# A two-stack transformer kernel: the order of VectorE's and ScalarE's work in mixer 1's tail, at mixer 2's entry and at the mixers' output

## The reference

```
x = x + 0.5 * rms(swiglu(rms(x)))          # feed-forward, width 2816
x = x + rms(token_mixing(rms(x) @ w_in))   # 6 heads band attention (A), 4 heads differential attention (B), 6 heads stick breaking (C)
x = x + 0.5 * rms(swiglu(rms(x)))
```

```
z = rms(h) @ w_in  ->  q, k, v, forget logit, a_val, a_gate, sc_b, sc_c, sc_x
y = [forgetting attention | silu(LN(dwconv31(a_val * sigmoid(a_gate)))) @ pw | sc_b * conv3(sc_c * sc_x)]
h = h + rms(head_rms(y) @ w_out);   h = h + rms(conv-swiglu(rms(h)))
```

## Time and profile before

| what | value |
|---|---|
| median of 3 runs | 3466.94 us (3461.26 to 3468.24) |
| the profiled execution's own time | 3464.3 us |
| its span | 3462.6 us |
| PE busy | 3362.6 us, 97% |
| DVE busy | 1761.5 us, 51% |
| ACT busy | 1413.3 us, 41% |
| POOL busy | 292.6 us, 8% |
| chain that ended last | PE 89%, DVE 5%, ACT 3% |
| mean granted TensorE clock | 0.99 |

### The profile page before, as it was taken

One profiled execution on the slowest core, in us unless ns is written; L12 is line 12 of the kernel. 1 busy time (PEld: TensorE's weight loads), 2 busy tenths in 40 slices (PEclk: granted clock), 3 DMA queues, 4 the chain that ended last, 5 costly groups with the idle time before them and its releaser, 6 DMA issues.

```text
span 3462.6 us, 52727 instructions
## 1 busy us (share of the span) xinstructions
PE 3362.6 (97%) x21230; PEld 2933.6 (85%) x21230; DVE 1761.5 (51%) x2408; ACT 1413.3 (41%) x2396; POOL 292.6 (8%) x159
## 2 busy tenths in 40 slices
PE   8999999899999999999899999999999999999999
PEld 7887876688889888876688888879999988799998
DVE  4443556554425442556554425745665267366643
ACT  3232445442224322446433224465443345654332
POOL 0000022100000000022100001210000022100000
PEclk9999999999999999999999999999999999999999
DMA  3333321223333332311223332112323322122222
GB/s 110 91 100 125 104 61 55 68 79 92 96 95 89 97 94 95 104 58 53 68 82 94 94 98 76 50 53 68 91 91 95 101 56 55 46 80 91 91 92 86
DMA packets 330735, 287.46 MB, mean 83 GB/s; under 512 B 9697, under 2 KB 326201, under 8 KB 330581
## 3 DMA queue, kind: packets, MB, share of 16 engines
q1 hardware_dynamic: 329444, 283.85, 27.3%
q10 hardware_dynamic: 1137, 1.42, 0.1%
HBM read 283.10 MB, written 5.27 MB: 83 GB/s over the span
## 4 chain that ended last, share of the span: by engine, by line
PE 89%; DVE 5%; ACT 3%; DMA 1%; issue 1%; ACTq 0%; POOL 0%; SPq 0%; DVEq 0%
PE ps L607 22%; PE ps L608 22%; PE ps L609 21%; PE ps L658 3%; PE ps L660 3%; PE ps L659 3%; PE ps L719 2%; PE ps L1829 1%; PE ps L1831 1%; PE ps L1830 1%; DVE m_aconv L2269 1%; PE ps L1417 1%; PE ps L723 1%; PE ps L1441 1%; PE ps L1456 1%
## 5 line engine op out<-in xcount | busy, mean ns | idle before, releaser
L607 PE MATMUL ps<-xhi,whi 128*128 128x512 f32 (+2 forms) x3088 | 1067.5, 346 | 18.2 <-DVE m_aconv L2220 13.1
L608 PE MATMUL ps<-xlo,whi 128*128 128x512 f32 (+2 forms) x3088 | 1058.1, 343 | 0.0
L599 DVE TENSOR_TENSOR wlo<-raw,whi 128x1024 fp32r<-128x1024 f32 (+1 forms) x410 | 495.2, 1208 | 1100.7 <-ACT whi L592 1098.2
L609 PE MATMUL ps<-xhi,wlo 128*128 128x512 f32 (+2 forms) x3088 | 1054.3, 341 | 0.0
L592 ACT ACTIVATE whi<-raw 128x1024 fp32r<-128x1024 f32 (+1 forms) x493 | 512.1, 1041 | 1143.2 <-PE ps L609 1031.7
L607 PEld LDWEIGHTS ps<-xhi,whi 128*128 128x128 f32 x3088 | 584.6, 189 | 104.2 <-issue 16.8
L609 PEld LDWEIGHTS ps<-xhi,wlo 128*128 128x128 f32 x3088 | 583.2, 189 | 69.6
L608 PEld LDWEIGHTS ps<-xlo,whi 128*128 128x128 f32 x3088 | 584.1, 189 | 66.1 <-issue 0.5
L607 PE MATMUL ps<-hhi,whi 128*128 128x512 f32 (+2 forms) x1056 | 358.9, 340 | 0.4 <-issue 0.4
L608 PE MATMUL ps<-hlo,whi 128*128 128x512 f32 (+2 forms) x1056 | 358.1, 339 | 0.0
L609 PE MATMUL ps<-hhi,wlo 128*128 128x512 f32 (+2 forms) x1056 | 357.7, 339 | 0.0
(11 more groups left out here) (287 smaller groups left out, 5141.2 us busy)
## 6 DMA issues: line engine op xcount, KB each, us to landing
raw<-in_ffn_w_up_dram SPq DMA_DIRECT2D x176, 512.0 KB, 3.7
raw<-in_ffn_w_down_dram SPq DMA_DIRECT2D x120, 512.0 KB, 3.4
raw<-in_w_in_dram SPq DMA_DIRECT2D x94, 512.0 KB, 3.8
raw<-in_ffn_w_gate_dram SPq DMA_DIRECT2D x88, 512.0 KB, 3.7
raw<-in_w_out_dram SPq DMA_DIRECT2D x32, 512.0 KB, 3.4
raw<-in_ffn_w_down_dram SPq DMA_DIRECT2D x24, 256.0 KB, 2.7
tbias_scratch<-rev_scratch SPq DMA_DIRECT2D x1, 3072.0 KB
y<-tbias_scratch SPq DMA_DIRECT2D x6, 512.0 KB, 4.6
```

The lines of the kernel that those rows point to most:

```text
L599: eng.tensor_tensor(lo[:, 0:n], raw[slot][:, 0:n], hi[:, 0:n].bitcast(F32), ALU.subtract).then_inc(b.s.weights_split, 1)
L607: pe.matmul(o, wh, hi[:, t0:t0 + w], start=first, stop=False)
L608: pe.matmul(o, wh, lo[:, t0:t0 + w], start=False, stop=False)
L609: ins = pe.matmul(o, wl, hi[:, t0:t0 + w], start=False, stop=last)
```

## The change

1. Mixer 1: `OUT_FILL` gives step 29 one output tile less (3 to 2) and step 33 one more (0 to 1). `B_NORM` is 23, so sums, logarithms, product and hi part of the B norm are each one step earlier; the lo part is at B_NORM+5, step 28 (before: 27).
2. Mixer 1, DVE: the evacuations and outputs of steps 27 and 30 (`DEFER1`) are done one step later, behind that step's `probabilities`. In step 27 this is the evacuation of granule 23 (pair 7's values), in step 30 the outputs of pair 6.
3. The lo split of granule 25 moves from POOL to DVE, step 30.
4. `act_out`, all mixers: `next_hi(0)` comes after `act_yevac` of m=1, and no longer before it.
5. Mixer 2's entry, PE: granule 4 waits for one evacuation, granule 5 for two (before: three and four). DVE evacuates granules 1 to 3 ahead of the forget chain, and gives `a_gate_in` before the forget lo part, both after evac(4).
6. Mixer 2, DVE: step 2 has three taps (2 and 1), step 3 four (1 and 3); the last three taps come in step 12.

```diff
--- before.py
+++ after.py
@@ -136,9 +136,11 @@
 
 
 LAG1 = 2
-OUT_FILL = [3, 3, 2, 2, 2, 0]
+OUT_FILL = [3, 2, 2, 2, 2, 1]
 OUT_TILES = [(24, t) for t in range(8)] + [(25, t) for t in range(4)]
-B_NORM = 24
+B_NORM = 23
+
+DEFER1 = (27, 30)
 
 
 def schedule1():
@@ -206,7 +208,7 @@
 FILL2 = [13, 13, 13, 13, 12] * 3 + [11, 11, 10]
 
 DW_OPS = [(t, c) for t in range(TAPS) for c in range(2)]
-DW_PER_STEP = 5
+DW_STEP = {2: (2, 1), 3: (1, 3)}
 
 
 def schedule2():
@@ -1132,10 +1134,11 @@
                 if j == nq * late - 1 and KIND[g][0] == "M":
                     for i in range(nq * late + (2 if KIND[g] == "M2" else 0), nq * DOWN_PAIRS):
                         hi_split(i)
-                    next_hi(0)
                 if j % nq == nq - 1:
                     act.wait_ge(b.s.granules_done, gb + j + 1 + CR)
                     act_yevac(act, b, g, j // nq, col)
+                if j == nq * late - 1 and KIND[g][0] == "M":
+                    next_hi(0)
             if KIND[g][0] == "F":
                 for i in range(nq * late + 2, nq * DOWN_PAIRS):
                     hi_split(i)
@@ -1717,16 +1720,19 @@
                     logits(st.sc)
                 if last is not None and KINDS[last // 4] == "B":
                     probabilities(last)
-                for g in st.done:
-                    if g < 24:
-                        evac(g)
-                for p_ in st.pairs:
-                    outputs(p_)
+                for n in ([n_step - 1] if n_step - 1 in DEFER1 else []) + ([n_step] if n_step not in DEFER1 else []):
+                    for g in STEPS1[n].done:
+                        if g < 24:
+                            evac(g)
+                    for p_ in STEPS1[n].pairs:
+                        outputs(p_)
+                if n_step == 30:
+                    split_lo(dve, b, mgb(l) + 25, 1, handover=True)
                 if n_step == B_NORM + 1:
                     dve.wait_ge(s.b_act_steps, l * 2 + 2)
                     dve.tensor_tensor(m1.ob[:, :, :], m1.ob[:, :, :], m1.rb[:, :, :],
                                       ALU.mult).then_inc(s.b_scaled, 1)
-                if n_step == B_NORM + 3:
+                if n_step == B_NORM + 5:
                     dve.wait_ge(s.b_scaled, l + 1)
                     dve.wait_ge(s.b_hi, l + 1)
                     dve.scalar_tensor_tensor(out=m1.olo[:, 3:5, :], in0=m1.ob[:, :, :],
@@ -1738,7 +1744,7 @@
 
         def pool_mix1(pool, l):
 
-            for g in range(5, 26):
+            for g in range(5, 25):
                 split_lo(pool, b1, mgb(l) + g, g % 2, handover=(g == 5))
 
 
@@ -1807,7 +1813,7 @@
                 if t == 0:
                     pe.wait_ge(s.weights_split, g2b(l) + g + 1 + CR)
                     if g >= 4:
-                        pe.wait_ge(s.columns_out, l * NCOL + g + CR - 1)
+                        pe.wait_ge(s.columns_out, l * NCOL + CR + {4: 1, 5: 2}.get(g, g - 1))
                 ins = tile_mm(pe, b, gbank(g), g % 2, t * P, xhi[:, t, :], xlo[:, t, :], t == 0, t == 7)
                 if t == 7:
                     ins.then_inc(s.granules_done, 1)
@@ -2281,7 +2287,8 @@
             evac(0)
             dve.wait_ge(s.columns_out, l * NCOL + 1 + CR)
             dve.tensor_scalar(m2.u, m2.u, bf[:, bass.ds(l, 1)], None, ALU.add).then_inc(s.forget_in, 1)
-            evac(1)
+            for g in range(1, 4):
+                evac(g)
 
             dve.wait_ge(s.forget_steps, l * 3 + 3)
             ch(dve.scalar_tensor_tensor(out=m2.lf, in0=m2.u, scalar=0.0, in1=m2.e, op0=ALU.min,
@@ -2292,17 +2299,16 @@
                                           0.0 if a == 0 else m2.nf[:, a - 1:a], ALU.mult, ALU.subtract))
                 ch.wait()
             dve.sem_inc(s.forget_sums, 1)
-            for g in range(2, 8):
+            for g in range(4, 8):
                 evac(g)
-                if g == 3:
+                if g == 4:
+                    dve.wait_ge(s.columns_out, l * NCOL + 5 + CR)
+                    dve.sem_inc(s.a_gate_in, 1)
                     dve.wait_ge(s.forget_hi, l + 1)
                     for a in (0, 64):
                         ins = dve.tensor_tensor(m2.nfx[a + 32:a + 40, :], m2.nf, m2.nfx[0:8, :].bitcast(F32),
                                                 ALU.subtract)
                     ins.then_inc(s.forget_lo, 1)
-                if g == 4:
-                    dve.wait_ge(s.columns_out, l * NCOL + 5 + CR)
-                    dve.sem_inc(s.a_gate_in, 1)
                 if g == 5:
                     dve.wait_ge(s.a_gate_done, l + 1)
                     ch(dve.tensor_tensor(apad[:, :, TAPS - 1:], apad[:, :, TAPS - 1:], aconv[:, :, :], ALU.mult))
@@ -2333,11 +2339,11 @@
                 if st.sc is not None:
                     largest(st.sc)
                 if n_step < LN_STEP:
-                    depthwise(2)
+                    depthwise(DW_STEP.get(n_step, (2, 3))[0])
                 for g, hf in st.halves:
                     evac_half(g, hf)
                 if n_step < LN_STEP:
-                    depthwise(DW_PER_STEP - 2)
+                    depthwise(DW_STEP.get(n_step, (2, 3))[1])
                 for g in st.done:
                     if SPLIT2_DVE <= g + 2:
                         split_lo(dve, b, g2b(l) + g + 2, g % 2, n_of(g + 2), handover=first_lo)
```

## The result

The changed kernel takes **3437.79 us** (median of 4 runs, 3436.86 to 3439.53) beside 3465.35 for the kernel before on the same chip: ratio 0.9922, 95% interval 0.9905 to 0.9939. That is 27.6 us less. Forecast were 3437 us and a sum of -28.5; the two profiled spans, 3462.6 and 3435.1, differ by 27.5. A second timing of the same file (the last experiment) gave 0.9926 (0.9913 to 0.9940). The ratio that I compare experiments with is the mean of the two, 0.9924; it is itself known to about 0.001, or 4 us.

A forecast was written before the change was run, and what follows sets the result against it. TensorE was taken to bound the kernel, busy 97% of the span, with about 100 us of waits to win. Terms -9.4 + 2.0 - 17.4 - 3.7 = -28.5 us against 3464.3 gave 3437 us, range about 3428 to 3453.

The forecast's parts named there:

- Part 1: Mixer 1's tail: the 4.5 us wait on unit 27's chain and its low clock go; -15.4 us for both layers.
- Cost nothing: Mixer 1, step 30: granule 25's lo split on DVE (about 1.2 us) falls into DVE's wait for unit 30's sigmoid.
- Part 2: Mixer 1's norm one step earlier: 1.68 us wait goes, 3.0 wait and 1.7 low clock come; +6.0 for both layers.
- I take that, 1.7: Low clock behind the new wait at the second norm sum: 1.7 us a layer, between 0 and 3.4.
- Part 3: Mixers' outputs: PE's wait for m=1 moves to the sum of squares; +2.0 us for both mixer 1, 0 in mixer 2.
- Part 4: Mixer 2's entry: the waits for evac(2) and the low clocks behind them go; -17.4 us for both layers.
- Part 5: Mixer 2's depthwise taps: step 3's 2.09 us wait goes, -4.2; late taps cost +0.5; -3.7 us for both layers.
- rival A: No new low clock behind the waits of parts 2 and 3: 6.8 us less, 3430 us; chance 0.20.
- B: Mixer 2's entry: the wait moves to granule 5 or 6, some 5 us a layer, 3447 us; chance 0.12.
- C: Unit 27's chain is bound by its sigmoid, the entry by something unseen; little gain left, 3463 us; chance 0.04.
- D: Mixer 1: the clock, down at the second norm sum, stays down in the tail; slower than before, 3470 us; chance 0.04.
- no low was longer than 7: Argument against D: no 8 us window lost more than 3.4 us, so no low clock lasted longer than 7 us.

The follow-up runs named there:

- the last experiment: The changed kernel unedited, timed again on the same chip as reference for the three kernels with both repairs: 3438.57 us, ratio 0.9926.
- logarithm first: Changed kernel, but ACT takes the first logarithm before the hi split of granule 22 and the second behind it: 3425.57 us, ratio 0.9899.

## Why the prediction was right

The time came within 1 us of the forecast. The mechanisms were right, but that closeness is luck: the terms missed by up to 4 us each and cancelled.

**Part 1, the tail: right.** Unit 27's chain ends ahead of PE, with the first operation at 0.42 where it had been 2.60. DVE's timeline in the changed kernel, unit 27's chain:

```profile
616.20 0.42 DVE L1666 TENSOR_TENSOR m_w<-m_w,later 128x256 f32<-128x256 f32 x1
...
620.28 0.42 DVE L1675 TENSOR_TENSOR m_w<-m_w,strict 128x256 f32<-128x256 f32 x1
```

The small terms held too: the B lo part is late by 0.24 (0.4 taken), the values' transposes by 0.78 (0.7), and the two later waits on DVE shrank from 0.94 and 1.43 to 0.62 and 0.67, 1.08 us (1.1 taken); the 0.62 is now a wait for ACT's copy, so no more was to be had there from DVE. "Cost nothing" for the moved split was right only because of the deferral, as the run without it showed.

**Part 2, the norm: mechanism right, one term too small.** The wait is 3.30 us (3.0 taken) and the 1.68 us wait is gone. The step that failed is "I take that, 1.7": the low clock behind it cost 3.4 and 3.2 us, the upper bound. I had priced it by the nearest wait in length, 3.11 us at an output; the low behind the 4.47 us wait in the same mixer was the better neighbour. The upper bound was no bound either. Eight traces have this wait of 3.30 us in both layers; the low cost 1.7 us once (five taps again, layer 0), 3.2 to 3.4 twelve times, and 4.5 to 4.8 three times (not deferred, layer 0; split on POOL, both). By the forecast, part 2 alone was already a loss of 3.0 us a layer. It is one of 4.9, and its cure is an order on ACT.
No row shows a gap at a table switch: the load follows the split at 583.12, and of the 35 loads in this trace all but the first begin 0.02 us behind the operation before them. PE's wait is 3.30 us, not the 4.4 that by estimate the drain in the Trainium skill (ScalarE: Activation LUTs, What ACT_TABLE_LOAD costs) would give.

**Part 3, the outputs: right in kind.** PE's wait moved to the sum of squares, 3.60 and 4.25 us in mixer 1 ("about 4") and 2.46 and 2.08 in mixer 2 ("about 2"). The low clock behind it in mixer 1 cost 1.7 and 2.6 us (1.7 taken), but it does not always follow: with the norm back in step 24 none came behind a wait of 3.42 us there (last section). For mixer 2 the term 0 left out the low clock behind 2.46 us (0.83 over 8 us, 1.4 us), which stood in the text as "at worst". What the forecast did not ask is what follows from its own finding: if `next_hi(2)`'s DMA holds the sum, then that is what to move. It was worth 15.9 us.

**Part 4, the entry: right to 0.1 us in the sum.** PE goes through granules 4 to 7 without a wait at a full clock. The narrow place was as tight as forecast. POOL's splits of granules 5 and 6 in the changed kernel:

```profile
2122.34 3.07 POOL L601 TENSOR_TENSOR wlo<-raw,whi 128x1024 fp32r<-128x1024 f32 x1 [55.26 <-ACT whi L594]
2128.00 2.55 POOL L601 TENSOR_TENSOR wlo<-raw,whi 128x1024 fp32r<-128x1024 f32 x1 [2.59 <-ACT whi L594]
```

DVE's evacuations of granules 4 and 5, which mark the ends of these granules on PE:

```profile
2125.70 0.71 DVE L2226 TENSOR_TENSOR m_aconv<-ps,r 128x528 f32<-128x528 f32 x1 [0.24 <-PE ps L611]
...
2131.59 0.71 DVE L2224 SCALAR_TENSOR_TENSOR m_q<-ps,r 128x528 f32<-128x528 f32 x1 [3.31 <-PE ps L611]
```

POOL's split of granule 5 ends at 2125.41, 0.1 us before PE takes it up at 2125.49, and that of granule 6 at 2130.55, a microsecond early. (The prediction's 2130.3 for granule 5 is 2124.6 + 5.8 = 2130.4.)

**Part 5, the taps: the wait right, the clock missed.** -6.3 instead of -3.7. The wait of 2.09 us had no low clock behind it in layer 0, which I cited, but it had one in layer 1, which I had not looked at. Kernel before:

```profile
2857.00:2865.00 8.00, 5.91 (x32) 3.99 (x30) 6.93 (x11) 4.34 (x13) 2.77 (x1) 0.79 0.29 82
```

That is 1.7 us. The same wait in layer 0, without a fall, was the one row cited in favour of rival A. The three late taps cost nothing that can be seen.

**The rivals.** A fell: a low clock followed the norm's waits of 3.30 us and three of the four new waits ahead of the sums of squares. B fell by 0.1 us: granule 5 was just in time. C and D fell; in each tail the one low is the 3.4 or 3.2 us at step 24, and from 593 to 676 us PE runs at 2.4 GHz. So the oscillation that the Trainium skill (TensorE: Matmul & The Clock Gate, A second HAM failure mode: psum-queue depth-cycling) describes did not set in, although six waits of 0.46 to 0.78 us stand between 626 and 644 us. The premise of D was off as well: in the steps before, from 589 to 626 us, PE has only two waits, 0.26 and 0.24 us, so this is no hard test of the rule. And "no low was longer than 7" read too much out of windows that begin behind the wait: over 2799 to 2815 us of the kernel before PEclk is 0.68, so that low lasted 10 us, some 4 of them in the wait, where they cost nothing.

## What to carry to other kernels

When an edit removes a wait, work out the whole chain of the next event that PE needs, and edit what ends last in it: an edit to the first of two waits in line measured 0 alone and 12 us once the second was gone. Before moving work into another step, write down which other instruction of the same engine waits for an event in that step, and put the short operation that releases PE ahead of it. Price a low clock from all occurrences of the same wait, in every layer, and let the sum carry it as a chance.

## What the runs showed of the hardware

- **The same wait falls on either side of the clock, and its length does not settle it.** PE's wait of 1.55 us at mixer 2's output granule was followed by 1.2 GHz in one layer and not in the other, in the kernel before (layer 0) and in the changed one (layer 1). So was the 2.09 us wait in the kernel before and in the run that brought it back. At mixer 1's sum of squares in layer 0 a wait of 3.36 us was followed by a low clock (logarithm first, 0.62 over the 8 us from 670), and one of 3.42 was not (norm in step 24):

```profile
671.00:679.00 8.00, 7.46 (x61) 7.44 (x62) 4.26 (x8) 3.84 (x11) 1.48 (x2) 1.00 0.05 16
```

Behind the 3.30 us waits the clock fell in every trace that has them. Between two traces of the changed kernel, with spans of 3435.1 and 3436.9, this moves single stages by 1.0 to 1.3 us.
- **A split on POOL stretches an SBUF operation that DVE begins during it**, in these cases by 2.0 to 2.2 us: the mask (2.60 instead of 0.42) in one order, the product (3.24 instead of 1.23) in another. It is one operation a split, and not always the first. In the changed kernel unit 26's mask began beside a split and took its usual 0.41; the running products behind it took 3.88, where the wider ones of unit 27 took 2.34:

```profile
610.49 2.67 POOL L601 TENSOR_TENSOR wlo<-raw,whi 128x1024 fp32r<-128x1024 f32 x1 [7.93 <-ACT whi L594]
...
610.50 0.41 DVE L1666 TENSOR_TENSOR m_w<-m_w,later 128x256 f32<-128x256 f32 x1
610.95 3.88 DVE L1669 TENSOR_TENSOR_SCAN m_scan<-m_w,ones 128x384 f32<-128x384 f32 x2
```
- **The table load did not wait for the data of the logarithm behind it.** In the run with the logarithm first it ran from 577.83 to 579.11, and the logarithm had its sum 0.57 us after that. Where ACT would idle it cost PE nothing.
